# Two transformer blocks on one core: three norms and the query rank are summed by one TensorE tile instead of two, and three warm-up matmuls stand where four stood

## The chip, the cores and the metric

The kernel runs on one core of one Trainium2 chip. The metric is the device time of the program in microseconds (us); lower is better.

## The reference, cut to what matters

Two transformer blocks follow each other over 512 tokens of 1024 features, in float32. The first has latent attention (a query rank of 256 and a key/value rank of 128, each with its own RMS norm), an mLSTM, a gated feed-forward and a gate on per-layer embeddings; the second has differential attention, forgetting attention and a squared-ReLU feed-forward. Every norm has this form:

```python
def rms_norm(x, g):
    xf = x.astype(jnp.float32)
    y = xf * lax.rsqrt(jnp.mean(xf * xf, axis=-1, keepdims=True) + EPS)
    return (y * g.astype(jnp.float32)).astype(x.dtype)

    u = rms_norm(h, attn_pre_norm[i])
    c_q, c_kv, k_rope, ... = split_cols(u @ w_in[i], IN_SIZES)
    q = (rms_norm(c_q, q_norm[i]) @ w_uq[i]).reshape(...)
    ...
    h = h + rms_norm(mix, attn_post_norm[i])
    ...
    x = x + rmsnorm(mix @ w_out[l], ln_attn_post[l])
    ...
    x = x + rmsnorm(u @ w_down[l], ln_mlp_post[l])
```

The change touches how the mean of squares is formed for four of these norms: `cq` (the query rank), `attn_post`, `post_2` and `mlp_post_2` (the three norms behind `w_out`, `w_out_2` and `w_down_2`).

## The kernel before

**Layout.** Features lie on the 128 partitions, tokens along the free axis. A tensor of 1024 features is `KD` = 8 tiles of 128x512 in `tiles` (SBUF). A float32 product is split into three matmuls (`three`, L902 to L904: high x high, low x high, high x low). ScalarE (ACT) rounds the high part, VectorE (DVE) subtracts it to get the low part (L2154, L2157). Weights come as `raw_slab` slabs of 128x1024 by DMA, two slots in turn; ACT makes `w_hi` (L1541), DVE makes `w_lo` (L2154), and TensorE (PE) waits for `slab_lo` before it uses the slab. Almost all time is PE working through these products.

**Order.** Nothing is scheduled automatically. Each engine has its own program, written out by hand, and executes it in order; engines wait for each other by counting semaphores. So a wait on an engine holds up all that stands behind it in that engine's program.

**A norm.** ACT squares each of the 8 tiles into `tiles[SQ]` or `tiles[SQ+1]` (semaphore `sq_done`). DVE adds each square to the sum tile `tiles[SSUM]` (`add_part`, L2207, or `add_square`, L2200; semaphore `ssum_done`). Then PE adds over the partitions: `stat` (from L1006) multiplies each tile of squares, as the stationary operand, with a matrix of ones taken from `cols` (`summed`, L1001; the matmul is L1003), one 128x128 product for each group of 128 tokens. ACT takes the root (L1567), DVE the reciprocal (L2232), and PE spreads the factors over the partitions (`spread`, L1033).

For the norms in `HALVED` (`attn_post`, `post_2`, `mlp_post_2`) the tokens are in two parts, `EARLY` (256 tokens) and `LATE` (256 tokens, norm name with `_b`), so that the early tokens' norm overlaps the late tokens' last matmuls. In these, DVE adds only the first seven tiles of squares. The eighth, `t(SQ + (KD - 1) % 2)`, goes to PE as a second tile, so `stat` issues two products for each 128 tokens and adds them in PSUM.

The query rank has two tiles, `cq0` and `cq1`. DVE copies them out (`rank_taken`), ACT squares them into `early[:, RANK_SQ[0]]` and `[1]` (L1699), and `stat("cq")` multiplies both with ones: 2 tiles x 4 groups of tokens. `stat("ckv")`, for the one tile of the key/value rank, follows at once. Both stand on PE behind the first dense projection (`mq0`) and ahead of the second (`mk0`).

**Start.** While the first weights and activations are loaded, PE multiplies zeros, `WARM` times (L1141), and then begins with `first_of_all` (L942 to L948), the first part of the product `mv`; the rest of `mv` (L902 to L904) goes over the 8 feature tiles k, with a new slab at every even k.

Of the kernel before, what the change touches and what calls it, by code (L numbers as in the profile page):

```python
# [20 lines left out]
ALU = mybir.AluOpType  # L21
# [3 lines left out]
P = 128  # L25
S = 512
ST = S // P
D = 1024
KD = D // P
# [5 lines left out]
ML_H, ML_D, ML_W, TAPS = 4, 128, 512, 4  # L35
# [22 lines left out]
CLAMP = 2.0 ** 58  # L58
OVERFLOWS = 2.0 ** 28.5
SMALLEST = 2.0 ** -50  # L60
WARM = 4


SLAB = 8
# [33 lines left out]
for _name, _n in [("attn_pre_norm", 8), ("attn_post_norm", 8), ("ffn_pre_norm", 8), ("ffn_post_norm", 8),  # L98
# [5 lines left out]
    NCOLS += _n  # L104


NORMS = ([("attn_pre", KD, KD - 1), ("cq", 2, 0), ("ckv", 1, 0), ("ml", ML_H, 0)]
         + [("attn_post", KD, KD), ("attn_post_b", 2, 1), ("ffn_pre", KD, KD - 1), ("ffn_post", KD, KD + 1), ("pre_2", KD, KD - 1)]
         + [("df", DF_H, 0)]
         + [("post_2", KD, KD), ("post_2_b", 4, 3), ("mlp_pre_2", KD, KD - 1), ("mlp_post_2", KD, KD), ("mlp_post_2_b", 1, 0)])  # L110
NORM_NO, SQ0, ADD0, RSTD0 = {}, {}, {}, {}
_sq = _add = NRSTD = 0
for _n, (_name, _t, _a) in enumerate(NORMS):
    NORM_NO[_name], SQ0[_name], ADD0[_name] = _n, _sq, _add
# [6 lines left out]
    _add += _a  # L121
ADDS = {name: a for name, _, a in NORMS}
SQUARES = {name: n for name, n, _ in NORMS}
BY_POOL = {"mlp_post_2": (0, 1, 2, 4, 5, 6), "mlp_post_2_b": (0, 1, 2, 4, 5)}
HALVED = ("attn_post", "post_2", "mlp_post_2")
EARLY, LATE = slice(0, S // 2), slice(S // 2, S)
# [3 lines left out]
def token_tiles(name):  # L130
    return range(ST // 2, ST) if name.endswith("_b") else range(ST // 2) if name in HALVED else range(ST)
# [112 lines left out]
RANK_RAW, RANK_SQ = (4, 5, 6), (12, 13, 14)  # L244
# [37 lines left out]
PROB, MO, TMP, SSUM, SQ, RSTD, NTILES = 0, 4, 8, 10, 11, 13, 14  # L282
# [6 lines left out]
def at(n, it, per):  # L289


    return it * per + n
# [294 lines left out]
def build(nc, xT, pT_in, pos_in, cols_in, square_in, onehot_in, relb_in, stream, out):  # L587
    scratch = nc.dram_tensor("bias_rows", [DF_H, S], F32, kind="Internal").ap()
    decay_rows = nc.dram_tensor("decay_rows", [ML_H, S], F32, kind="Internal").ap()
    with ExitStack() as ctx:  # L590
# [9 lines left out]
        early = nc.alloc_sbuf_tensor_at("early", [P, SET, S], F32, offset=arena_at + -arena_at % 32)  # L600
# [25 lines left out]
        def t(n):  # L626
            return tiles[:, n]
# [7 lines left out]
        sem = Semaphores(lambda name: ctx.enter_context(nc.semaphore(name)))  # L635
# [256 lines left out]
        def _(pe):  # L892
            def claim(key):

                b, before, _ = uses[key]
                if before:
                    pe.wait_ge(*before)
                return bank[b]
# [16 lines left out]
            def u(k):  # L915
                return u_hi[:, k], u_lo[:, k]
# [84 lines left out]
            def summed(o, c, square_, first, last):  # L1001

                return pe.matmul(o[:, c:c + P], square_, ones, start=first, stop=last)  # L1003

            def stat(name):

                o = claim(("stat", name))
                if name == "cq":
                    pe.wait_ge(sem.sq_done, SQ0[name] + 2)
                    for i in range(ST):  # L1010
                        for k in range(2):
                            last = summed(o, i, early[:, RANK_SQ[k], i * P:(i + 1) * P], k == 0, k == 1)
                    last.then_inc(sem.stat_ready, 1)
                    return
                squares = [early[:, RANK_SQ[2]] if name == "ckv" else t(PROB if name in ("ffn_pre", "pre_2", "mlp_pre_2") else SSUM)]
                if ADDS[name]:
                    pe.wait_ge(sem.ssum_done, ADD0[name] + ADDS[name])
                if "post" in name or not ADDS[name]:
                    pe.wait_ge(sem.sq_done, SQ0[name] + SQUARES[name])
                if "post" in name and name != "ffn_post":  # L1020
                    squares.append(t(SQ + (KD - 1) % 2))
                for i in token_tiles(name):
                    for n, square_ in enumerate(squares):
                        last = summed(o, i, square_[:, i * P:(i + 1) * P], n == 0, n == len(squares) - 1)
                last.then_inc(sem.stat_ready, 1)
# [113 lines left out]
            pe.wait_ge(sem.warm_set, 1)  # L1139
            for n in range(WARM):  # L1140
                pe.matmul(bank[STAT_BANK][:, :], warm.to_broadcast([P, P]), warm.to_broadcast([P, S]), start=True, stop=True)  # L1141
# [10 lines left out]
            for n, name in enumerate(DENSE):  # L1152
# [7 lines left out]
                elif n == 7:  # L1160
                    o = claim("gate_cols")
                    pe.wait_ge(sem.gate_scanned, 1)
                    for c in range(2):
                        for i in range(ST):
                            at_ = (c * ST + i) * ML_H
                            last = pe.transpose(o[:, at_:at_ + ML_H], tiles[0:ML_H, TMP + c, i * P:(i + 1) * P], square[0:ML_H, 0, 0:ML_H])
# [172 lines left out]
            for n in range(2):  # L1339
                slot = arrived("proj", n)  # L1340
                for m in range(4):
                    last = features(f"proj{4 * n + m}", slot, 2 * m, [u(6), u(7)])
# [56 lines left out]
            for n in range(KD // 2):  # L1399
                slot = arrived("fv", n)  # L1400
                for k in (2 * n, 2 * n + 1):
                    for i in range(ST):
                        o = claim(f"fv{i}") if k == 0 else bank[uses[f"fv{i}"][0]]
                        x = [part_[:, k, i * P:(i + 1) * P] for part_ in (u_hi, u_lo)]
                        last = three(o[:, :], x, slab(0, slot, (k % 2) * ST, S), k == 0, k == KD - 1)
# [101 lines left out]
            for c, part_ in enumerate(PARTS):  # L1507
                o = claim(("last", c))
                for k in range(HALF2):
# [3 lines left out]
                    last = three(o[:, part_], slab(0, slot, k % SLAB), pair(k, HALF2 + k, cols_=part_), k == 0, k == HALF2 - 1)  # L1513
# [10 lines left out]
            for i in token_tiles("mlp_post_2_b"):  # L1524
                last = summed(late, i * P, t(SQ + (KD - 1) % 2)[:, i * P:(i + 1) * P], False, i == ST - 1)
# [618 lines left out]
        def _(dve):  # L2144
# [8 lines left out]
            def tt(o, a, b, op):  # L2153
                return nc.vector.tensor_tensor(o, a, b, op)  # L2154
# [10 lines left out]
            def slab_lo(s, it=0, step=0):  # L2165

                s += 1
                if isinstance(it, int) and at(s, it, step) >= NSLABS:
                    return
                dve.wait_ge(sem.slab_hi, at(s + 1, it, step))  # L2170
                low(w_lo[:, s % 2], raw[:, s % 2], w_hi[:, s % 2]).then_inc(sem.slab_lo, 1)
# [35 lines left out]
            def add_part(name, n, m, part_):  # L2207

                dve.wait_ge(sem.sq_done, SQ0[name] + n + 1)
                dve.wait_ge(sem.ssum_done, ADD0[name] + n + (not name.endswith("_b")))  # L2210
                tt(tiles[:, SSUM, part_], tiles[:, SSUM, part_], tiles[:, SQ + m % 2, part_], ALU.add).then_inc(sem.ssum_done, 1)
# [13 lines left out]
            def inverse_root(name):  # L2225

                n = RSTD0[name]
                dve.wait_ge(sem.root_done, NORM_NO[name] + 1)
                if name not in ("ml", "df"):
                    i = token_tiles(name)  # L2230
                    own = slice(i[0], i[-1] + 1)
                    nc.vector.reciprocal(rstds[:, n, own], roots[:, n, own]).then_inc(sem.rstd_done, 1)  # L2232
                    return
                every = rstds[:, n:n + 4].rearrange("p h n -> p (h n)")
                if name == "ml":
                    nc.vector.reciprocal(every, every).then_inc(sem.rstd_done, 1)
                    return
                link(nc.vector.reciprocal(every, every))
                stt(every, every, 1.0 / OVERFLOWS, every, ALU.is_gt, ALU.mult).then_inc(sem.rstd_done, 1)
# [219 lines left out]
            o = full(dve, "rg")  # L2459
# [12 lines left out]
            def rank_taken(n):  # L2472
                tt(early[:, RANK_RAW[n]], full(dve, ("cq0", "cq1", "ckv")[n])[:, :], t(RSTD), ALU.mult).then_inc(sem.rank_copied, 1)
# [9 lines left out]
            tt(tiles[low_rows, TMP], tiles[low_rows, TMP], tiles[low_rows, RSTD], ALU.mult).then_inc(sem.rope_added, 1)  # L2483
            slab_lo(SLAB0["ckv"])
            rank_taken(1)
            for n in range(2):
                operand_lo(f"kpe{n}", arena[n * ROPE:(n + 1) * ROPE, A_KPE_L], tiles[low_rows, TMP], arena[low_rows, A_KPE_H])
            dve.wait_ge(sem.gate_log, 1)
# [3 lines left out]
            dve.wait_ge(sem.r_done, 1)  # L2492
            rank_taken(2)
            slab_lo(SLAB0[DENSE[0]])
            dve.wait_ge(sem.operand_lo, SPLIT_NO["kpe1"] + 1)
            link(nc.vector.tensor_tensor_scan(m, r, r, 0.0, ALU.max, ALU.max))
            tt(bm, m, a, ALU.add).then_inc(sem.gate_scanned, 1)
# [24 lines left out]
            for i, name in enumerate(DENSE):  # L2522
# [9 lines left out]
                acc, o = conv_tile(n), conv_input(n)  # L2532
# [138 lines left out]
            for m in range(KD - 2):  # L2671
                out_lo(OUT1, m + 2)
                add_part("attn_post", m, m, slice(0, S))
                if m + 1 < GROUP:
                    aside_lo(FIRST["glu"][m + 1])
            add_part("attn_post", KD - 2, KD - 2, EARLY)
            inverse_root("attn_post")

            def late_attn_post(c, k):
# [236 lines left out]
            def ob(m, c, part_):  # L2916

                o = full(dve, ("ob", m, c))
                if m == 0:
                    dve.wait_ge(sem.part_kept, KD)  # L2920
                tt(tiles[:, m, part_], o[:, part_], part[:, m, part_], ALU.add).then_inc(sem.out_summed, 1)
# [16 lines left out]
            for m in range(5, KD):  # L2938
                ob(m, 0, EARLY)
                add_part("post_2", m - 1, m - 1, EARLY)  # L2940
            ob(4, 1, LATE)
            inverse_root("post_2")
            ob(5, 1, LATE)
# [67 lines left out]
            def last_sum(c, part_):  # L3011

                o = full(dve, ("last", c))
                tt(tiles[:, KD - 1, part_], tiles[:, KD - 1, part_], o[:, part_], ALU.add).then_inc(sem.half_added, 1)

            last_sum(0, EARLY)
            inverse_root("mlp_post_2")
            done = H0["mlp_post_2"]
            for c, (name, part_) in enumerate((("mlp_post_2", EARLY), ("mlp_post_2_b", LATE))):
# [157 lines left out]
```

## Time and profile before

| | |
|---|---|
| time, median of 3 runs | 1284.31 us (1283.98 to 1284.41) |
| the profiled execution | 1284.02 us |
| its span in the profile | 1282.2 us (1.8 us lie around it) |
| PE busy | 1268.9 us, 99% of the span |
| DVE busy | 766.5 us, 60% |
| ACT busy | 549.3 us, 43% |
| chain that ended last | PE 95%, DVE 3%, ACT 1%, issue 1% |

PE is the engine for matmuls and PEld its weight loads, which run beside them. Each float32 product with ones shows as two records, called two passes here: 88 products, 176 records. A record of a matmul includes the way through the array, so that in a train the spacing of the starts, not the duration, says what one costs. The ends of matmuls are modelled.

### The profile page before, as it was taken

To read this page: it belongs to the slowest core of one execution; us is meant where nothing else is said; L and a number is where in the kernel's file an instruction comes from. 1 tells how busy PE (TensorE), PEld (TensorE's weight loads), DVE (VectorE), ACT (ScalarE), POOL (GpSimd) and SP (SyncE) were. 2 spreads that over 40 slices of the span, in tenths; PEclk is the share of its full clock that TensorE was granted. 3 is DMA by queue.
4 is the path that set the end of the run, shared out by engine and by line. 5 is a ranking of instruction groups with operands and counts; after the bars stand their busy time and mean duration, and the time that the engine had idled before them with its cause. 6 is when DMAs were issued, how large, how long until landed. Compare 5 with 4: busy or idle time off the path is not lost.

```text
span 1282.2 us, 17439 instructions
## 1 busy us (share of the span) xinstructions
PE 1268.9 (99%) x6386; PEld 1072.7 (84%) x6386; DVE 766.5 (60%) x1250; ACT 549.3 (43%) x921; POOL 32.5 (3%) x42
## 2 busy tenths in 40 slices
PE   9999999999999999999999999999999999999997
PEld 7887888988888888888888888888988888888886
DVE  6777895655444443323685896898868422455334
ACT  6656865433222223232564655667443222222221
POOL 0010000000000000000000000000000000000002
PEclk9999999999999999999999999999999999999999
DMA  5232113122223223332333323423122322222332
GB/s 199 85 130 83 34 36 130 34 76 89 98 98 98 98 90 124 102 111 98 99 104 110 99 83 93 114 79 112 50 66 85 112 92 92 96 98 98 99 99 82
DMA packets 37563, 120.97 MB, mean 94 GB/s; under 512 B 4600, under 2 KB 6776, under 8 KB 37504
## 3 DMA queue, kind: packets, MB, share of 16 engines
q1 hardware_dynamic: 35888, 116.93, 28.3%
q0 software_dynamic: 896, 2.64, 0.7%
q8 instruction: 39, 0.64, 0.2%
q10 hardware_dynamic: 720, 0.59, 0.1%
q14 instruction: 20, 0.16, 0.0%
HBM read 112.79 MB, written 2.11 MB: 90 GB/s over the span
## 4 chain that ended last, share of the span: by engine, by line
PE 95%; DVE 3%; ACT 1%; issue 1%; DVEq 0%; ACTq 0%
PE bank L902 29%; PE bank L903 29%; PE bank L904 29%; PE bank L1003 2%; PE bank L1096 1%; DVE arena L2157 1%; PE bank L1423 1%; PE bank L1125 0%; PE bank L1141 0%; PE bank L1383 0%; PE bank L1382 0%; DVE tiles L2154 0%; PE bank L1033 0%; PE bank L1073 0%; DVE tiles L2157 0%
## 5 line engine op out<-in xcount | busy, mean ns | idle before, releaser
L2154 DVE TENSOR_TENSOR w_lo<-raw_slab,w_hi 128x1024 fp32r<-128x1024 f32 (+1 forms) x199 | 243.6, 1224 | 269.1 <-ACT w_hi L1541 264.6
L902 PE MATMUL bank<-u_hi,w_hi 128*128 128x512 f32 x824 | 322.8, 392 | 0.0
L904 PE MATMUL bank<-u_hi,w_lo 128*128 128x512 f32 x824 | 321.0, 390 | 0.0
L903 PE MATMUL bank<-u_lo,w_hi 128*128 128x512 f32 x824 | 320.9, 389 | 0.0
L1541 ACT ACTIVATE w_hi<-raw_slab 128x1024 fp32r<-128x1024 f32 x197 | 207.7, 1054 | 183.8 <-PE bank L904 181.3
L902 PE MATMUL bank<-arena,w_hi 128*128 128x512 f32 (+1 forms) x692 | 260.9, 377 | 0.0
L903 PE MATMUL bank<-arena,w_hi 128*128 128x512 f32 (+1 forms) x692 | 259.3, 375 | 0.0
L904 PE MATMUL bank<-arena,w_lo 128*128 128x512 f32 (+1 forms) x692 | 259.3, 375 | 0.0
L904 PEld LDWEIGHTS bank<-u_hi,w_lo 128*128 128x128 f32 x824 | 154.7, 188 | 32.4
L902 PEld LDWEIGHTS bank<-u_hi,w_hi 128*128 128x128 f32 x824 | 154.7, 188 | 31.7 <-issue 0.9
L903 PEld LDWEIGHTS bank<-u_lo,w_hi 128*128 128x128 f32 x824 | 154.8, 188 | 30.7
L904 PEld LDWEIGHTS bank<-arena,w_lo 128*128 128x128 f32 x692 | 130.2, 188 | 23.5
L902 PEld LDWEIGHTS bank<-arena,w_hi 128*128 128x128 f32 x692 | 130.3, 188 | 23.2 <-DVE w_lo L2154 0.3
L903 PEld LDWEIGHTS bank<-arena,w_hi 128*128 128x128 f32 x692 | 130.3, 188 | 22.0
L2154 DVE TENSOR_TENSOR tiles<-tiles 128x512 f32<-128x512 f32 (+2 forms) x129 | 86.6, 672 | 33.3 <-ACT tiles L1826 19.9
L2154 DVE TENSOR_TENSOR tiles<-bank,tiles 128x512 f32<-128x512 f32 (+2 forms) x75 | 51.3, 688 | 65.0 <-PE bank L904 62.1
L2154 DVE TENSOR_TENSOR arena<-tiles,arena 128x512 f32 (+3 forms) x88 | 59.1, 674 | 26.5 <-ACT arena L1875 20.3
L2103 ACT ACTIVATE arena<-tiles 128x512 f32 (+1 forms) x32 | 20.2, 630 | 100.2 <-DVE tiles L2154 100.2
L1654 ACT ACTIVATE tiles<-bank,negmax 128x128 f32<-128x128 f32 (+3 forms) x80 | 41.8, 524 | 36.8 <-DVE negmax L2364 35.7
L1875 ACT ACTIVATE arena<-tiles 128x512 f32 (+1 forms) x22 | 13.9, 632 | 81.5 <-DVE tiles L2154 81.5
L1634 ACT ACTIVATE probsT<-bank 128x128 fp32r<-128x128 f32 (+1 forms) x80 | 35.0, 437 | 24.8 <-PE bank L1096 24.5
L902 PE MATMUL bank<-u_hi,arena 128*128 128x256 f32 (+3 forms) x144 | 42.9, 298 | 0.8 <-DVE u_lo L2157 0.8
(275 smaller groups left out, 1451.5 us busy)
## 6 DMA issues: line engine op xcount, KB each, us to landing
raw_slab<-in_stream SPq DMA_DIRECT2D x197, 512.0 KB, 3.3
aside_raw<-in_stream SPq DMA_DIRECT2D x8, 512.0 KB, 5.2
arena<-arena SPq DMA_DIRECT2D x32, 128.0 KB, 2.3
residual<-in_xT SPq DMA_DIRECT2D x8, 256.0 KB, 5.6
out_hT<-residual SPq DMA_DIRECT2D x12, 128.0 KB, 1.8
arena<-forget_rows SPq DMA_DIRECT2D x8, 128.0 KB, 2.4
raw_slab<-in_stream SPq DMA_DIRECT2D x2, 256.0 KB, 3.3
early<-decay_rows POOLq DMA_DIRECT2D x2, 256.0 KB, 3.8
```

Of the source, the lines that this page charges most:

```text
L902: pe.matmul(o, ws[0], xs[0], start=first, stop=False)
L903: pe.matmul(o, ws[0], xs[1], start=False, stop=False)
L904: return pe.matmul(o, ws[1], xs[0], start=False, stop=last)
L1003: return pe.matmul(o[:, c:c + P], square_, ones, start=first, stop=last)
L1096: last = pe.transpose(o[:, j * P:(j + 1) * P], tiles[:, src, j * P:(j + 1) * P], ident)
L1423: pe.matmul(o[:, 0:w], arena[:, FX_TILES[p][queries][j], i * P:w], arena[:, FX_TILES[p][keys][j], 0:w], start=queries == "q", stop=False)
L1541: nc.scalar.activation(w_hi[:, s % 2], raw[:, s % 2], ACT.Copy).then_inc(sem.slab_hi, 1)
L1634: nc.scalar.activation(transposed(0, v % ST), by_key_tile(o, w), ACT.Copy).then_inc(sem.pT_hi, 1)
L1654: nc.scalar.activation(tiles[:, PROB + exp_slot(a, n, j), 0:w], o[:, 0:w], ACT.Exp, bias=negmax[:, e:e + 1], accum_out=rowsum[:, e:e + 1]) ...
L1875: nc.scalar.activation(arena[:, at(m, it, 2)], t(SQ + m), ACT.Copy).then_inc(sem.hidden_hi, 1)
L2103: nc.scalar.activation(arena[:, at(i, it, 2)], t(SQ + i), ACT.Copy).then_inc(sem.hidden_hi, 1)
L2154: return nc.vector.tensor_tensor(o, a, b, op)
```

## The change

`WARM` goes from 4 to 3. The three halved norms get one more addition on DVE: the eighth tile of squares, early tokens only, is added to `SSUM` as soon as ACT has squared it, and `stat` takes only `SSUM` for the early tokens (the late tokens keep their two tiles). For `cq`, DVE adds the two tiles of squares in place, and `stat` takes the one sum; its wait changes from `sq_done` to `ssum_done`. The numbers in `NORMS` are the count of tiles and of additions.

```diff
-WARM = 4
+WARM = 3
...
-NORMS = ([("attn_pre", KD, KD - 1), ("cq", 2, 0), ("ckv", 1, 0), ("ml", ML_H, 0)]
-         + [("attn_post", KD, KD), ("attn_post_b", 2, 1), ("ffn_pre", KD, KD - 1), ("ffn_post", KD, KD + 1), ("pre_2", KD, KD - 1)]
+NORMS = ([("attn_pre", KD, KD - 1), ("cq", 2, 1), ("ckv", 1, 0), ("ml", ML_H, 0)]
+         + [("attn_post", KD, KD + 1), ("attn_post_b", 2, 1), ("ffn_pre", KD, KD - 1), ("ffn_post", KD, KD + 1), ("pre_2", KD, KD - 1)]
          + [("df", DF_H, 0)]
-         + [("post_2", KD, KD), ("post_2_b", 4, 3), ("mlp_pre_2", KD, KD - 1), ("mlp_post_2", KD, KD), ("mlp_post_2_b", 1, 0)])
+         + [("post_2", KD, KD + 1), ("post_2_b", 4, 3), ("mlp_pre_2", KD, KD - 1), ("mlp_post_2", KD, KD + 1), ("mlp_post_2_b", 1, 0)])
...
             def stat(name):
 
                 o = claim(("stat", name))
-                if name == "cq":
-                    pe.wait_ge(sem.sq_done, SQ0[name] + 2)
-                    for i in range(ST):
-                        for k in range(2):
-                            last = summed(o, i, early[:, RANK_SQ[k], i * P:(i + 1) * P], k == 0, k == 1)
-                    last.then_inc(sem.stat_ready, 1)
-                    return
-                squares = [early[:, RANK_SQ[2]] if name == "ckv" else t(PROB if name in ("ffn_pre", "pre_2", "mlp_pre_2") else SSUM)]
+                ranks = {"cq": RANK_SQ[0], "ckv": RANK_SQ[2]}
+                squares = [early[:, ranks[name]] if name in ranks else t(PROB if name in ("ffn_pre", "pre_2", "mlp_pre_2") else SSUM)]
                 if ADDS[name]:
                     pe.wait_ge(sem.ssum_done, ADD0[name] + ADDS[name])
                 if "post" in name or not ADDS[name]:
                     pe.wait_ge(sem.sq_done, SQ0[name] + SQUARES[name])
-                if "post" in name and name != "ffn_post":
+                if name.endswith("_b"):
                     squares.append(t(SQ + (KD - 1) % 2))
...
             rank_taken(1)
+            rank_squares = early[:, RANK_SQ[0]], early[:, RANK_SQ[1]]
...
             rank_taken(2)
             slab_lo(SLAB0[DENSE[0]])
+            dve.wait_ge(sem.sq_done, SQ0["cq"] + 2)
+            tt(rank_squares[0], rank_squares[0], rank_squares[1], ALU.add).then_inc(sem.ssum_done, 1)
             dve.wait_ge(sem.operand_lo, SPLIT_NO["kpe1"] + 1)
...
             add_part("attn_post", KD - 2, KD - 2, EARLY)
+            add_part("attn_post", KD - 1, KD - 1, EARLY)
             inverse_root("attn_post")
...
                 add_part("post_2", m - 1, m - 1, EARLY)
+            add_part("post_2", KD - 1, KD - 1, EARLY)
             ob(4, 1, LATE)
             inverse_root("post_2")
...
             last_sum(0, EARLY)
+            add_part("mlp_post_2", KD - 1, KD - 1, EARLY)
             inverse_root("mlp_post_2")
```

DVE at the query rank, before. The rows follow each other; `early_50<-bank0` is `rank_taken(2)`, the `w_lo` behind it is the weight slab of `mk0`, and the 4x512 rows are the gates of the mLSTM.

```order
L2154 TENSOR_TENSOR arena<-tiles,arena 64x512 [waits operand_hi] x2
L2157 SCALAR_TENSOR_TENSOR tiles<-tiles 4x512 [waits gate_log]
L2490 SCALAR_TENSOR_TENSOR tiles<-tiles 4x512 [waits dve_step]
L2154 TENSOR_TENSOR tiles<-tiles 4x512 [waits dve_step]
L2154 TENSOR_TENSOR early_50<-bank0,tiles 128x512 [waits slab_used,r_done]
L2154 TENSOR_TENSOR w_lo<-raw_slab,w_hi 128x1024 [waits slab_hi]
L2496 SCALAR_TENSOR_TENSOR tiles<-tiles 4x512 [waits operand_lo]
```

The same place on DVE after the change:

```order
L2148 TENSOR_TENSOR arena<-tiles,arena 64x512 [waits operand_hi] x2
L2151 SCALAR_TENSOR_TENSOR tiles<-tiles 4x512 [waits gate_log]
L2485 SCALAR_TENSOR_TENSOR tiles<-tiles 4x512 [waits dve_step]
L2148 TENSOR_TENSOR tiles<-tiles 4x512 [waits dve_step]
L2148 TENSOR_TENSOR early_50<-bank0,tiles 128x512 [waits slab_used,r_done]
L2148 TENSOR_TENSOR w_lo<-raw_slab,w_hi 128x1024 [waits slab_hi]
L2148 TENSOR_TENSOR early_50<-early_50 128x512 [waits sq_done]
L2493 SCALAR_TENSOR_TENSOR tiles<-tiles 4x512 [waits operand_lo]
```

The new addition stands behind `rank_taken(2)` and behind the low part of the slab.

PE at the query rank, before: the end of `mq0`, the two sums, the start of `mk0`.

```order
L904 MATMUL bank1<-u_hi,w_lo 128x512
L1003 MATMUL bank7<-cols,early_50 128x128 [waits sq_done,rstd_copied]
L1003 MATMUL bank7<-cols,early_50 128x128 x7
L1003 MATMUL bank4<-cols,early_50 128x128 [waits sq_done,rope_read]
L1003 MATMUL bank4<-cols,early_50 128x128 x3
L902 MATMUL bank2<-u_hi,w_hi 128x512 [waits operand_lo,slab_lo]
```

The same place on PE after the change:

```order
L904 MATMUL bank1<-u_hi,w_lo 128x512
L1003 MATMUL bank7<-cols,early_50 128x128 [waits ssum_done,rstd_copied]
L1003 MATMUL bank7<-cols,early_50 128x128 x3
L1003 MATMUL bank4<-cols,early_50 128x128 [waits sq_done,rope_read]
L1003 MATMUL bank4<-cols,early_50 128x128 x3
L902 MATMUL bank2<-u_hi,w_hi 128x512 [waits operand_lo,slab_lo]
```

Eight products with ones became four, and the first of them waits for `ssum_done`.

DVE near the end of the program after the change (`mlp_post_2`), with the new row in the third place. Before the change the same rows stood there without it.

```order
L2148 TENSOR_TENSOR tiles<-tiles 128x512 [waits ssum_done,sq_done]
L2148 TENSOR_TENSOR tiles<-tiles,bank 128x256 [waits part_done]
L2148 TENSOR_TENSOR tiles<-tiles 128x256 [waits ssum_done,sq_done]
L2226 RECIPROCAL rstds<-rstds 128x2 [waits root_done]
L2151 SCALAR_TENSOR_TENSOR tiles<-tiles,cols,bank 128x256 [waits spread_ready]
```

The new addition follows the last sum of tile 7 (`part_done`) and stands ahead of the reciprocal.

## Rows read from the trace of the kernel before

**Rows 1.** The page: busy time by engine, then the chain by engine.

```profile
PE 1268.9 (99%) x6386; PEld 1072.7 (84%) x6386; DVE 766.5 (60%) x1250; ACT 549.3 (43%) x921; POOL 32.5 (3%) x42
...
PE 95%; DVE 3%; ACT 1%; issue 1%; DVEq 0%; ACTq 0%
```

**Rows 2.** Timeline of the start: start us, duration us, engine, line, instruction, [idle before].

```profile
3.65 0.34 PEld L1141 LDWEIGHTS bank<-small 128*128 128x128 f32 x1 [0.52 <-issue]
...
4.51 0.20 PEld L1141 LDWEIGHTS bank<-small 128*128 128x128 f32 x1 [0.52 <-issue]
4.57 0.72 ACT L1666 ACTIVATE u_hi<-residual,cols 128x512 fp32r<-128x512 f32 x1
4.95 0.19 PEld L1141 LDWEIGHTS bank<-small 128*128 128x128 f32 x1 [0.24 <-issue]
...
5.82 0.19 PEld L942 LDWEIGHTS bank<-w_hi,u_hi 128*128 128x128 f32 x1 [0.24 <-issue]
```

**Rows 3.** Timeline, slab 2 of `mv` arrives and feature tile k = 4 begins.

```profile
14.45 1.06 ACT L1541 ACTIVATE w_hi<-raw_slab 128x1024 fp32r<-128x1024 f32 x1 [2.08 <-DMA raw_slab<-in_stream]
...
15.54 1.22 DVE L2154 TENSOR_TENSOR w_lo<-raw_slab,w_hi 128x1024 fp32r<-128x1024 f32 x1 [1.12 <-ACT w_hi L1541]
...
16.95 0.19 PEld L902 LDWEIGHTS bank<-w_hi,u_hi 128*128 128x128 f32 x1
```

**Rows 4.** Timeline, where the engines last wait for PE ahead of the rank.

```profile
34.69 1.06 ACT L1541 ACTIVATE w_hi<-raw_slab 128x1024 fp32r<-128x1024 f32 x1 [0.81 <-PE bank L904]
```

**Rows 5.** Timeline around the two sums of the ranks.

```profile
52.03 0.63 ACT L1699 ACTIVATE early<-early 128x512 f32<-128x512 f32 x1 [3.84 <-DVE early L2154]
...
56.96 2.87 PEld L1003 LDWEIGHTS bank<-cols,early 128*128 128x128 f32 x24
...
57.32 0.69 DVE L2154 TENSOR_TENSOR early<-bank,tiles 128x512 f32<-128x512 f32 x1
57.93 1.22 DVE L2154 TENSOR_TENSOR w_lo<-raw_slab,w_hi 128x1024 fp32r<-128x1024 f32 x1
58.05 0.63 ACT L1699 ACTIVATE early<-early 128x512 f32<-128x512 f32 x1 [3.12 <-DVE early L2154]
59.06 1.21 DVE L2496 TENSOR_TENSOR_SCAN tiles<-tiles 4x512 f32<-4x512 f32 x1
...
59.76 0.19 PEld L902 LDWEIGHTS bank<-u_hi,w_hi 128*128 128x128 f32 x1
```

**Rows 6.** Timeline at the sum of `attn_post`.

```profile
235.13 0.38 ACT L1835 ACTIVATE tiles<-bank 128x256 f32<-128x256 f32 x1 [2.22 <-PE bank L904]
...
236.25 0.98 PEld L1003 LDWEIGHTS bank<-cols,tiles 128*128 128x128 f32 x8
237.16 0.19 PEld L902 LDWEIGHTS bank<-arena,w_hi 128*128 128x128 f32 x1
```

**Rows 7.** Timeline at the sum of `post_2`.

```profile
910.82 0.42 ACT L2056 ACTIVATE tiles<-tiles 128x256 f32<-128x256 f32 x1 [0.85 <-DVE tiles L2154]
...
911.49 0.98 PEld L1003 LDWEIGHTS bank<-cols,tiles 128*128 128x128 f32 x8
```

**Rows 8.** Timeline at the sums of `mlp_post_2`, early and late tokens.

```profile
1265.09 0.42 DVE L2154 TENSOR_TENSOR tiles<-tiles,bank 128x256 f32<-128x256 f32 x1 [2.78 <-PE bank L904]
1265.54 0.42 ACT L2135 ACTIVATE tiles<-tiles 128x256 f32<-128x256 f32 x1 [4.57 <-DVE tiles L2154]
...
1266.21 0.98 PEld L1003 LDWEIGHTS bank<-cols,tiles 128*128 128x128 f32 x8
...
1270.30 0.61 PE L1003 MATMUL bank<-cols,tiles 128*128 128x128 f32 x4
...
1273.30 0.71 PE L1003 MATMUL bank<-cols,tiles 128*128 128x128 f32 x4 [0.96 <-ACT tiles L2135]
```

**Rows 9.** Busy time and granted clock of one stretch, PE first, PEclk behind POOL.

```profile
180.00:190.00 10.00, 8.72 (x65) 7.99 (x64) 9.86 (x25) 6.82 (x20) 0.00 (x0) 1.00 0.07 28
```

**Rows 10.** Who waited for whom, PEld: us in total, times, longest us.

```profile
PEld bank L1003 <- ACT tiles L2135: 1.2, 1, 1.2
```

## Prediction

> **What bounds the kernel now.** I read the page first, then who waited for whom, then the timeline at each place that the diff touches. PE is busy for 99% of the span, and the chain that ended last runs 95% through it [rows 1]. So a microsecond that PE's own program gains or loses is in general one of the span, and work on DVE or ACT costs nothing as long as PE does not wait for it. The question at each place is therefore twofold: how many passes does PE lose, and is DVE's new addition done when PE gets there?
>
> A pass with ones costs what the spacing says. At `attn_post` eight weight loads of L1003 begin at 236.25 and the next product's load at 237.16 [rows 6], so 0.91 / 8 = 0.114 us each. A 128x128 product is two passes.
>
> A wait ahead of such passes costs a little more than its length, since the first weight load is no longer hidden: four passes took 0.61 us where they followed other matmuls and 0.71 us behind a wait [rows 8]. I count 0.10 us for each new wait. From the end of one engine's instruction to the start of one that waited for it there are 0.03 us (DVE ends at 1265.09 + 0.42 = 1265.51, ACT begins at 1265.54) [rows 8].
>
> **Warm-up: about -0.2 us.** At the start the loads of L1141 are 0.86 us apart (3.65 to 4.51), and from 4.51 on 0.44 us (4.51 to 4.95) [rows 2]: TensorE ran at 1.2 GHz there and at 2.4 GHz behind it. The removed matmul is the last one, two passes at the higher level, 0.87 us. What follows can't gain all of it: `u_hi` of the first tile ends only at 4.57 + 0.72 = 5.29 [rows 2], and further on PE meets the DMA. Slab 2 comes late (ACT waited 2.08 us for its DMA), its low part ends at 15.54 + 1.22 = 16.76, and PE takes it at 16.95 [rows 3]. None of that depends on PE, so whatever PE has gained, it can't begin k = 4 before 16.79: a gain of 0.16. The bounds are 0 and 0.4 (the load there may be partly hidden anyway); I take 0.2, near the row's own number. The gain then travels on: ACT waits for PE at 34.69 [rows 4], and DVE's chain up to the rank hangs from there without a pause that could hide 0.2 us.
>
> **The query rank: about +1.9 us.** Four products go, 8 passes. But the addition stands on DVE behind `rank_taken(2)` and the low part of `mk0`'s slab, and DVE begins what now follows those at 59.06 [rows 5]. The squares are long there (52.03 + 0.63 = 52.66), so nothing but the place in the program holds it. The trace has no such addition in `early`, but a DVE tensor-tensor of 128x512 f32 takes 0.69 us here [rows 5]. So `ssum_done` comes at 59.06 + 0.69 = 59.75, and PE's first load at 59.78, where before it stood at 56.96. PE then has the 8 passes of `cq` and the 8 of `ckv`: 16 x 0.114 = 1.82, and 0.10 for the wait: `mk0` begins at 61.70. Before it was 59.76 [rows 5]. That is +1.94. The bounds: +1.5, if DVE's addition is only 0.6 us and the wait costs nothing more, with a DVE that runs somewhat earlier; +2.1 if the passes are spaced as in the whole train of 24 (2.80 / 24 = 0.117) and the restart is slower. Queued behind the wait on PE are `stat("ckv")`, whose own square was ready at 58.05 + 0.63 = 58.68, and all dense projections; the roots and the conversions of later slabs wait for PE in turn. DVE's gate scans move back by 0.6 us. They serve a product of PE six projections later, so that is covered.
>
> **attn_post: -0.45 us.** ACT's square ends at 235.13 + 0.38 = 235.51, DVE is idle, the addition of 128x256 takes 0.42 us (as the sum at 1265.09) [rows 6, 8]: ready at 235.96, ahead of PE's load at 236.25. Four passes go, 4 x 0.114. The cover is 0.29 us; without it the loss would be what it is at the next two.
>
> **post_2: -0.1 us.** The last square ends at 910.82 + 0.42 = 911.24 [rows 7]; with 0.03, the addition 0.42 and 0.03 PE may start at 911.72, and would have at 911.49. So it waits 0.23, plus 0.10, against 0.45 saved: -0.12.
>
> **mlp_post_2: -0.1 us.** The same sum: 1265.54 + 0.42 + 0.03 + 0.42 + 0.03 = 1266.44 against 1266.21 [rows 8], 0.33 lost and 0.45 saved: -0.12. The tail behind PE's last matmuls only moves with it, for its DVE work begins with PE's spread.
>
> The sum: -0.2 + 1.94 - 0.45 - 0.12 - 0.12 = **+1.05 us**. The profiled execution took 1284.02 us, 0.29 below the median of the runs, so it would take 1285.1, and the median **1285.4 us**.
>
> **The rivals.**
>
> *The clock falls in the wait at the rank.* PE would stand still for 59.78 - 57.0, some 2.8 us. The longest wait of PEld that the trace names is 1.2 us [rows 10], and in a stretch in which PE was busy for only 8.72 of 10 us the granted clock read 1.00 [rows 9], so no row shows what a pause of 2.8 us does. If the clock went to 1.2 GHz, the start shows the price: work ran at half rate from 0.93 to 4.51, 3.6 us, half of which, 1.8 us, is lost. That gives +2.85, 1287.2 us, slower. It decides from +2.57 us on. The Trainium skill (TensorE: Matmul & The Clock Gate, Part 1: The HAM clock gate) has the clock fall back to half after TensorE has been idle, and speaks for this case in kind; the pauses that this trace has did not bring it about.
>
> *The shift of the rank is taken up.* In the first attention PE waits for ACT and DVE (8.72 of 10 us busy, DVE 9.86) [rows 9]. If those engines' work there did not hang on PE's delayed products, the 1.94 would vanish there and so would the warm-up's 0.2: -0.7, 1283.6 us. Against it: their inputs are projections that PE makes behind the rank.
>
> *No wait at the rank.* If DVE reached the addition in time, 20 passes at 0.114 = 2.3 us and 0.2 would go: 1281.8 us, just inside the bound, and 1281.2 if the warm-up gave all of its 0.87, faster. Against it stands DVE's order and the row at 59.06.
>
> **How the numbers follow.** A measurement of this kernel tells about 0.2% (2.57 us) from no change. The forecast of +1.05 has a chance of 0.76, the clock 0.10, the shift taken up 0.10, no wait 0.04. The forecast alone spans 1284.4 to 1286.6 by its terms' bounds; to leave out no more than 2 in 10, I reach down to the case of 1283.6 and a little up: 1283.6 to 1286.8. Faster by over 0.2% has 0.03 (part of the last case), slower 0.11 (the clock and the forecast's upper edge), no change 0.86.
>
> **What the profile after would show.** A wait of PEld at L1003 on a DVE addition of some 2.8 us near 57 to 60, and the loads of `mk0` starting at about 61.5 (61.7 less the warm-up's gain); eight passes for `cq` and `ckv` each. Loads 0.22 us apart right behind them, if the clock holds; 0.43 if not. At `attn_post` no wait and four passes; at the other two a wait of some 0.2 us. The first load of k = 4 at about 16.8, with a wait for DVE. Wrong would be the prediction, if the delay at the rank is not found again at the first glu products (near 241.7), or if the passes behind the wait are slower.

## The result and the profile after

The changed kernel takes 1286.79 us (median of 22 runs, 1284.73 to 1287.61); the kernel before, beside it, 1284.59 us (22 runs, 1283.61 to 1285.27). The ratio is 1.0014, with a 95% interval from 1.0008 to 1.0021: slower by 0.14%, about 2 us, but under the 0.2% that I had set as the bound of no change.

The 22 runs are not one group. Seven lie between 1284.73 and 1285.65 us (median 1285.34) with a mean granted clock of TensorE of 0.998 of full speed; fifteen lie between 1286.56 and 1287.61 us (median 1286.87) with 0.996 or 0.997. Nothing lies between. The profiled execution (1285.34 us, span 1283.5) is of the lower group, so its trace shows the change without what makes the upper one. That trace first.

The page of the changed kernel, busy time and chain, answers to [rows 1]:

```profile
PE 1267.2 (99%) x6364; PEld 1069.8 (83%) x6364; DVE 768.4 (60%) x1254; ACT 549.8 (43%) x921; POOL 32.5 (3%) x42
...
PE 93%; DVE 4%; ACT 2%; issue 1%; DMA 0%; SPq 0%; ACTq 0%; DVEq 0%
```

PE has 22 records fewer (10 products with ones and one warm-up matmul, two passes each) and 1.7 us less to do, yet the span is 1.3 us longer. The chain now goes through DVE for 4% instead of 3%.

The timeline of the changed kernel at the query rank (start, duration, engine, line, instruction, [idle before]) answers to [rows 5]:

```profile
57.59 0.69 DVE L2148 TENSOR_TENSOR early<-bank,tiles 128x512 f32<-128x512 f32 x1
...
58.20 1.22 DVE L2148 TENSOR_TENSOR w_lo<-raw_slab,w_hi 128x1024 fp32r<-128x1024 f32 x1
...
59.33 0.69 DVE L2148 TENSOR_TENSOR early<-early 128x512 f32<-128x512 f32 x1
...
60.13 1.86 PEld L1003 LDWEIGHTS bank<-cols,early 128*128 128x128 f32 x16 [2.94 <-issue]
60.16 2.02 PE L1003 MATMUL bank<-cols,early 128*128 128x128 f32 x16 [2.54 <-DVE early L2148]
...
61.91 0.19 PEld L902 LDWEIGHTS bank<-u_hi,w_hi 128*128 128x128 f32 x1
```

The addition is the row at 59.33, behind `rank_taken(2)` and behind the slab, and ends at 60.02. PE's loads stood still for 2.94 us, and its matmuls for 2.54. Sixteen passes then fill 60.13 to 61.91, after which `mk0` begins, 2.15 us later than before. Of these, 0.27 came from the start of the program, so the rank cost 1.9.

The timeline of the changed kernel at `attn_post` and `post_2`, answers to [rows 6, 7]:

```profile
237.71 0.42 DVE L2148 TENSOR_TENSOR tiles<-tiles 128x256 f32<-128x256 f32 x1 [2.46 <-ACT tiles L1829]
238.42 0.54 PEld L1003 LDWEIGHTS bank<-cols,tiles 128*128 128x128 f32 x4
...
912.96 0.43 DVE L2148 TENSOR_TENSOR tiles<-tiles 128x256 f32<-128x256 f32 x1 [0.15 <-ACT tiles L2050]
913.46 0.52 PEld L1003 LDWEIGHTS bank<-cols,tiles 128*128 128x128 f32 x4 [0.21 <-issue]
```

At `attn_post` the new addition is done at 238.13 and PE comes at 238.42 without a pause; at `post_2` PE pauses for 0.21 us. `mlp_post_2` reads like `post_2`, again with 0.21 us.

To see where time goes I use the starts of the sums with ones as marks, since they stand in all versions; they are taken from the chain that ended last, written out in order of time. Each column is a stretch between two of them, so what happened ahead of it drops out: from `attn_pre` to `ml` (it holds the query rank), and from `ml` to the last of `mlp_post_2_b` (it holds the three norms).

| profile | `attn_pre` at | to `ml` | against before | to the last sum | against before |
|---|---|---|---|---|---|
| before | 26.18 | 145.37 | | 1101.75 | |
| after | 26.45 | 147.27 | +1.90 | 1100.91 | -0.84 |

### The profile page after: what moved, and what is told of

It is laid out like the page before. It is cut to its first block, busy times and chain, and to the rows that moved or that the text cites. A ratio compares the mean times of both kernels' runs of the same rounds, so it can differ in the third digit from the quotient of the medians.

```text
span 1283.5 us, 17402 instructions
## 1 busy us (share of the span) xinstructions
PE 1267.2 (99%) x6364; PEld 1069.8 (83%) x6364; DVE 768.4 (60%) x1254; ACT 549.8 (43%) x921; POOL 32.5 (3%) x42
## 4 chain that ended last, share of the span: by engine, by line
PE 93%; DVE 4%; ACT 2%; issue 1%; DMA 0%; SPq 0%; ACTq 0%; DVEq 0%
PE bank L902 28%; PE bank L903 28%; PE bank L904 28%; PE bank L1003 1%; PE bank L1090 1%; DVE tiles L2148 1%; DVE arena L2151 1%; PE bank L1417 1%; DVE w_lo L2148 0%; PE bank L1119 0%; DVE tiles L2151 0%; PE bank L1377 0%; DMA residual<-in_xT 0%; PE bank L1376 0%; PE bank L1067 0%
```

## The experiments

Every time is a median; the kernel before was run beside each. The first four ran on one chip (before: 1284.65 us, 33 runs), the next four on a second (1284.62, 27 runs), the last three on a third (1284.52, 27 runs).

### after_again: the changed kernel, for a profile of the upper group

> The changed kernel once more. Its runs so far lie in two groups, 7 at 1284.7 to 1285.7 us with a mean granted clock of 0.998 and 15 at 1286.6 to 1287.6 us with 0.996 or 0.997; its one profile was of the lower group. Theory A (the clock falls for a while in or behind the wait of 2.9 us that TensorE now has at the query rank): both groups come again, and a profile of the higher group shows matmuls behind the rank 0.43 us apart instead of 0.22, over some 3 us. Theory B (three warm-up matmuls leave TensorE idle for 0.8 us at the start, and the clock rises later): a profile of the higher group is slow at the start, not at the rank.

Measured: 1286.54 us (11 runs; four at 1285.39 to 1285.69, seven at 1286.19 to 1287.35), ratio 1.0012 (1.0003 to 1.0021). The profile, of 1286.19 us, has the mean clock 0.996 of the upper group.

Stretches of this profile, busy time of PE, PEld, DVE, ACT, POOL, then the granted clock, the DMA share and GB/s:

```profile
56.00:60.00 4.00, 1.46 (x7) 0.94 (x6) 3.93 (x6) 2.12 (x3) 0.53 (x1) 0.91 0.02 4
60.00:63.00 3.00, 3.00 (x17) 3.00 (x17) 2.96 (x4) 1.00 (x2) 0.00 (x0) 0.55 0.55 175
63.00:66.00 3.00, 3.00 (x16) 2.46 (x15) 2.13 (x6) 0.97 (x2) 0.00 (x0) 1.00 0.55 168
```

The same stretches of the first profile of the changed kernel, in the lower group:

```profile
56.00:60.00 4.00, 1.62 (x8) 1.00 (x6) 3.93 (x6) 1.66 (x3) 0.53 (x1) 1.00 0.01 4
60.00:63.00 3.00, 2.83 (x21) 2.68 (x22) 2.97 (x5) 2.23 (x4) 0.00 (x0) 1.00 0.49 175
```

And the loads of the sums in the timeline of after_again:

```profile
59.68 3.28 PEld L1003 LDWEIGHTS bank<-cols,early 128*128 128x128 f32 x16 [2.94 <-issue]
62.88 0.19 PEld L902 LDWEIGHTS bank<-u_hi,w_hi 128*128 128x128 f32 x1
```

The wait is the same 2.94 us. But toward its end the clock fell to 1.2 GHz and stayed there for about 3.4 us. (The stretches say so: 0.91 over 4 us is 0.7 us at half speed, 0.55 over 3 us is 2.7 us.) The sixteen passes took 3.20 us (59.68 to 62.88) instead of 1.78 (60.13 to 61.91). From `attn_pre` to `ml` the profile has 148.64 us, 1.37 more than the first one, and the medians of the two groups in the main comparison are 1.53 apart. At the start, where theory B put the cause, this profile is 0.45 us earlier than the other. Theory B falls for this profile; rank_only tests it over several runs. One half of what I expected missed: the slow matmuls are the sums themselves, not the products of `mk0`, for the fall began before the wait was over.

### rank_filled: the wait filled with matmuls over zeros

```diff
             def stat(name):
                 o = claim(("stat", name))
+                if name == "cq":
+                    for n in range(3):
+                        pe.matmul(bank[STAT_BANK][:, :], warm.to_broadcast([P, P]), warm.to_broadcast([P, S]), start=True, stop=True)
```

> The changed kernel with three more matmuls over zeros (128x512, six passes, 2.6 us) on TensorE just ahead of the sum for the query rank, into the bank that the sum then overwrites: they fill the wait and shift nothing, since TensorE would wait there. Theory A: the group at 1286.9 us is gone, all runs near 1285.3 us with clock 0.998. Theory B: both groups stay, 15 of 22 or so in the upper one. If the fill is a little too long, both get up to 0.1 us more.

Measured: 1285.28 us (1285.04 to 1285.71, 11 runs), ratio 1.0005 (0.9996 to 1.0014), the time of the lower group and no run above it. The stretches of its profile:

```profile
56.00:60.00 4.00, 4.00 (x14) 2.45 (x14) 3.90 (x5) 1.28 (x2) 0.52 (x1) 1.00 0.01 4
60.00:63.00 3.00, 3.00 (x21) 2.44 (x20) 2.97 (x5) 2.21 (x5) 0.00 (x0) 1.00 0.56 175
```

PE is now busy throughout, and the clock holds at 1.00; that it held in the other runs too is read from their times. DVE's addition comes as late as ever (147.21 us from `attn_pre` to `ml`, +1.84), only the second price of the wait is gone. It is TensorE standing still that lets the clock fall here, not the lateness of the addition as such.

### rank_sooner: the addition ahead of the slab

```diff
             rank_taken(2)
+            dve.wait_ge(sem.sq_done, SQ0["cq"] + 2)
+            tt(rank_squares[0], rank_squares[0], rank_squares[1], ALU.add).then_inc(sem.ssum_done, 1)
             slab_lo(SLAB0[DENSE[0]])
-            dve.wait_ge(sem.sq_done, SQ0["cq"] + 2)
-            tt(rank_squares[0], rank_squares[0], rank_squares[1], ALU.add).then_inc(sem.ssum_done, 1)
```

> The changed kernel with the addition for the query rank one place earlier on VectorE, ahead of the low part of the slab for mk0 instead of behind it. The addition should end near 58.9 on the scale of the profile after (58.20 + 0.69), not 60.02, so TensorE waits 1.8 us instead of 2.9 and mk0 begins 1.1 us sooner. Theory A: lower group 1284.2 us, and the upper group rarer or gone, since the pause is shorter. Theory B: both groups as often as before, 1.1 us lower. Rival for the wait itself: if the low part of the slab, now 0.6 us later, or the square of the key/value rank ends last, mk0 gains less than 1.1 us.

Measured: 1283.84 us (1283.55 to 1284.24, 11 runs), ratio 0.9994 (0.9985 to 1.0003), one group. The timeline:

```profile
58.17 0.68 DVE L2148 TENSOR_TENSOR early<-early 128x512 f32<-128x512 f32 x1
...
58.97 1.86 PEld L1003 LDWEIGHTS bank<-cols,early 128*128 128x128 f32 x16 [1.80 <-issue]
```

One place on DVE is worth 1.16 us by the marks (146.11 against 147.27), about the slab's 1.13 (58.20 to 59.33 above). With a pause of 1.80 us no run lies in an upper group, and every mean clock is 0.997 or 0.998, so the clock fell in none of the 11. Against the lower group the median is 1.5 lower, 0.4 more than the marks give; that rest is not accounted for, and the start varies by more (below).

### rank_undone: no change at the rank

```diff
-NORMS = ([("attn_pre", KD, KD - 1), ("cq", 2, 1), ("ckv", 1, 0), ("ml", ML_H, 0)]
+NORMS = ([("attn_pre", KD, KD - 1), ("cq", 2, 0), ("ckv", 1, 0), ("ml", ML_H, 0)]
...
+                if name == "cq":
+                    pe.wait_ge(sem.sq_done, SQ0[name] + 2)
+                    for i in range(ST):
+                        for k in range(2):
+                            last = summed(o, i, early[:, RANK_SQ[k], i * P:(i + 1) * P], k == 0, k == 1)
+                    last.then_inc(sem.stat_ready, 1)
+                    return
...
-            dve.wait_ge(sem.sq_done, SQ0["cq"] + 2)
-            tt(rank_squares[0], rank_squares[0], rank_squares[1], ALU.add).then_inc(sem.ssum_done, 1)
```

> The change without its part at the query rank (both tiles of squares go to TensorE again, no addition on VectorE there); three warm-up matmuls and the three norms as changed. From the differences of the two traces the norms give -0.45, -0.2 and -0.2 us. Theory A: no wait, one group of runs, clock 0.998 in all, about 1283.7 us if the start costs nothing, 1284.0 if the shorter warm-up costs the 0.27 us that the profile after showed there. Theory B: two groups 1.5 us apart remain, at 1283.7 and 1285.2.

Measured: 1283.40 us (1282.91 to 1283.57, 11 runs), ratio 0.9991 (0.9981 to 1.0000), one group: 3.1 us below the changed kernel on the same chip (after_again), and 0.3 below the 1283.7 that I expected. The marks say 145.33 and 1100.97: the rank's stretch is back where it was (-0.04), the norms' gain is kept (-0.78).

### rank_later: the addition behind the gate scan

```diff
             link(nc.vector.tensor_tensor_scan(m, r, r, 0.0, ALU.max, ALU.max))
             tt(bm, m, a, ALU.add).then_inc(sem.gate_scanned, 1)
+            dve.wait_ge(sem.sq_done, SQ0["cq"] + 2)
+            tt(rank_squares[0], rank_squares[0], rank_squares[1], ALU.add).then_inc(sem.ssum_done, 1)
```

(The two lines are taken away from their place ahead of the scan.)

> The changed kernel with the addition for the query rank three places later on VectorE, behind the two steps of the gate scan: it should begin 1.8 us later, so TensorE waits some 4.7 us instead of 2.9 and the lower group would be at 1287.2 us. Theory A: the clock falls in every run and, since the wait is longer, mostly while TensorE stands still, so the time is between 1287.5 and 1289 us with no run in a group of 0.998. Theory B: 1287.2 and 1288.7 us as often as before.

Measured: 1288.96 us (1288.54 to 1289.98, 6 runs), ratio 1.0033 (1.0021 to 1.0046). No run has a clock above 0.996. The loads of the sums and three stretches of its profile, which is of the slowest of the six runs:

```profile
61.82 3.49 PEld L1003 LDWEIGHTS bank<-cols,early 128*128 128x128 f32 x16 [4.77 <-issue]
...
60.00:63.00 3.00, 1.15 (x5) 1.18 (x6) 2.97 (x5) 1.05 (x1) 0.00 (x0) 0.70 0.48 175
63.00:66.00 3.00, 3.00 (x15) 2.90 (x14) 0.68 (x3) 0.62 (x3) 0.00 (x0) 0.50 0.44 168
66.00:69.00 3.00, 3.00 (x11) 2.34 (x10) 2.37 (x4) 0.61 (x1) 0.00 (x0) 0.66 0.02 7
```

The pause is 4.77 us here, and the clock stays down about twice as long as in after_again, about 6.8 us by the same working, well into `mk0`. The median lies at the upper edge of the 1287.5 to 1289 us that I expected, and for another reason: I had the clock low mostly while TensorE stands still, but it fell only at 61.2 us, 0.6 us ahead of the load at 61.82, and nearly all of the low stretch was work. The stretch from `attn_pre` to `ml` has 152.03 us in this profile, +6.66 against before. The wait itself explains about 3.7 (1.9, and 1.8 for the later place), the clock the other 2.9.

### rank_only: the rank's change on the kernel before, four warm-up matmuls

The diff is the rank's part of the change alone: `("cq", 2, 1)`, the new `squares` for `cq` in `stat`, and the addition on DVE.

> The kernel before with the change at the query rank alone, four warm-up matmuls. Theory A: two groups of runs, one 1.9 us above the kernel before (1286.5 us), one a further 1.4 to 1.6 us up (1288.0 us), though the warm-up is the old one. Theory B (the warm-up makes the upper group): one group only, at 1286.5 us.

Measured: 1287.98 us (10 runs; three at 1285.69 to 1285.83, seven at 1287.94 to 1288.72), ratio 1.0022 (1.0013 to 1.0032). The two groups are there with the old warm-up, and their medians are 2.3 apart. So the shorter warm-up does not make them: theory B falls here for good. Its profile (1288.10 us) has 148.84 us from `attn_pre` to `ml`, +3.47 and near after_again's +3.27, so the clock's share at the rank is at most 0.2 us larger here; that the lower group lies 0.7 below the 1286.5 I expected is not explained by a profile, since none was taken in it.

### warm_only: three warm-up matmuls, nothing else

```diff
-WARM = 4
+WARM = 3
```

> The kernel before with three warm-up matmuls instead of four and nothing else. Theory A (what follows the warm-up soon waits for the DMA of slab 2, so only 0.2 to 0.3 us arrive): a median 0.2 to 0.4 us below the kernel before, one group of runs. Theory B (the shorter warm-up costs, since TensorE idles before its first real matmul): 0.3 us or more above it, or a second group of runs some 1.5 us higher.

Measured: 1283.71 us (1283.31 to 1284.59, 11 runs) against 1284.62, 0.9 us lower where I expected 0.2 to 0.4; the ratio, 0.9996 (0.9987 to 1.0005), does not by itself tell it from no change. Theory B, that the shorter warm-up costs time or makes a second group, has nothing for it: the 11 runs have no group 1.5 us up. A likely reason why it gave more than I expected is in the next profile.

### norms_only: the three norms, four warm-up matmuls

The diff is that of the three norms: `KD + 1` in `NORMS`, `name.endswith("_b")` in `stat`, and the three `add_part(..., KD - 1, KD - 1, EARLY)`.

> The kernel before with the change to the three norms alone (four warm-up matmuls, query rank as before). By the marks in the traces the parts give 0.45, 0.2 and 0.2 us: 0.85 us below the kernel before, so near 1283.8 us. If the extra additions on VectorE cost TensorE more elsewhere than at these places, the gain is below 0.5 us. With rank_undone at 1283.4 us, the difference between the two is the warm-up's share.

Measured: 1283.94 us (1283.06 to 1284.48, 11 runs), 0.7 us below the kernel before, ratio 0.9994 (0.9985 to 1.0003). The marks give 145.38 and 1100.92 us: -0.83 from the norms and nothing at the rank. And its profile, of the slowest of the 11 runs, shows what the one profile of before did not: a start in which the clock rose late.

```profile
3.65 0.34 PEld L1142 LDWEIGHTS bank<-small 128*128 128x128 f32 x1 [0.52 <-issue]
4.51 0.34 PEld L1142 LDWEIGHTS bank<-small 128*128 128x128 f32 x1 [0.52 <-issue]
5.36 0.34 PEld L1142 LDWEIGHTS bank<-small 128*128 128x128 f32 x1 [0.52 <-issue]
6.21 0.34 PEld L1142 LDWEIGHTS bank<-small 128*128 128x128 f32 x1 [0.52 <-issue]
6.98 0.19 PEld L942 LDWEIGHTS bank<-w_hi,u_hi 128*128 128x128 f32 x1 [0.43 <-issue]
...
9.96 0.19 PEld L902 LDWEIGHTS bank<-w_hi,u_hi 128*128 128x128 f32 x1
```

The loads are 0.85 us apart until 6.21, where in [rows 2] they are 0.44 apart from 4.51 on. So the fourth warm-up matmul ran almost wholly at the lower level (5.36 to 6.98, 1.6 us for its two passes), and the first real matmul's load came at 6.98 instead of 5.82, though its operands were ready before 5.4. In the profile of warm_only it comes at 5.46:

```profile
4.17 0.19 PEld L1141 LDWEIGHTS bank<-small 128*128 128x128 f32 x1 [0.24 <-issue]
5.46 0.76 PEld L942 LDWEIGHTS bank<-w_hi,u_hi 128*128 128x128 f32 x4 [1.10 <-ACT w_hi L1669]
```

### best_again, norms_warm2, norms_warm0: how many warm-up matmuls

All three are rank_undone, with `WARM` at 3, 2 and 0.

> The version with three warm-up matmuls and the three norms changed, query rank as before, once more beside shorter warm-ups on one chip: 1283.4 us again, 0.8 to 1.3 us below the kernel before, in one group.

> The same with two warm-up matmuls (four passes, which end near 4.3 us while the clock is still at its lower level in most profiles). The first real matmul can't start before 5.3 us in any case (the activations are rounded then). Theory A (a warm-up matmul costs only where it runs past 5.3 us, and the clock needs work ahead of it to rise): no gain against three, and where the clock has not risen the pause of 1 us lets it rise later: 1283.4 to 1285 us. Theory B (warm-up matmuls are only in the way): 1283.0 us or less.

> The same with no warm-up matmuls. Theory A: the first real matmuls run at the lower level from 5.4 us on until the clock rises, some 3 to 7 us later; but the DMA of slab 2 hides a part of the 1.7 to 3.4 us that this costs, so 1284 to 1287 us. Theory B: 1283.0 us or less.

| `WARM` | us, median of 11 | range | ratio to before |
|---|---|---|---|
| 3 | 1283.39 | 1282.82 to 1283.95 | 0.9990 (0.9981 to 0.9999) |
| 2 | 1284.00 | 1283.01 to 1284.75 | 0.9995 (0.9986 to 1.0004) |
| 0 | 1284.28 | 1283.64 to 1285.31 | 0.9998 (0.9989 to 1.0007) |

The timeline of norms_warm0 at its first matmuls:

```profile
5.45 1.35 PEld L942 LDWEIGHTS bank<-w_hi,u_hi 128*128 128x128 f32 x4 [5.45 <-issue]
6.90 1.61 PEld L945 LDWEIGHTS bank<-w_lo,u_hi 128*128 128x128 f32 x4
8.60 0.97 PEld L948 LDWEIGHTS bank<-w_hi,u_lo 128*128 128x128 f32 x4
```

The first eight real matmuls run at about half speed there (3.15 us from 5.45 to 8.60, against 1.74 from 5.46 to 7.20 in the profile of warm_only), but the median is only 0.9 us above that with three. I take it that the waits for data that follow at the start give the rest back; no run tests that. All three lie where I expected them (with 2 and 0 by theory A); theory B, with 1283.0 us or less for both, falls. Three is the best of the counts tried, by medians whose ranges overlap. The version with three, the norms changed and the rank as before, is the fastest of the study: 1283.40 and 1283.39 us on two chips, 1.1 to 1.3 us (0.1%) below the kernel before, and 3.1 below the changed one on the same chip.

## Why the prediction was right, and where it was not

**The time lay in the range and the class was right, but the likeliest case was not the commonest.** I forecast 1285.4 us from a sum of +1.05 and gave the fall of the clock a chance of 1 in 10. The sum describes the lower group (1285.34 us) to within 0.1. But 15 of 22 runs were of the rival, 1286.87 us, and these set the median, which rose by 2.2 us where I had +1.05. That 1286.79 lies in my range at all is luck: the range ends at 1286.8, and the bounds that I named for the terms add up to no more than +1.7, which is 1286.1 us and not the 1286.6 that I gave. The rest was padding, and the rival's own 1287.2 us I had left outside. One sign that I named for being wrong, slower passes behind the wait, came in the upper group. The step that failed is the weight given to that rival. I had its mechanism, its place and the gap of 2.8 us in hand (2.94 measured), but took the 1.2 us pauses of the trace and a clock of 1.00 in them as evidence against it, though they said nothing about a pause over twice as long. Its price was 1.4 to 1.5 us, not 1.8: of the 3.4 us at the lower level in after_again 0.4 passed while TensorE was still idle, and half of the other 3.0 is 1.5.

**The rank, +1.94 predicted.** +1.90 by the marks in the lower group. The place on DVE's program decided it: the addition at 59.33 on the new scale, 0.27 later than 59.06, as the start was. Without the wait the loads would have begun at 57.23 (56.96 and the 0.27), so they came 2.90 late; the 24 passes had taken 2.80 (56.96 to 59.76) and the 16 took 1.78, so 1.02 of it was saved again.

**attn_post, -0.45 predicted.** From its sum to that of `attn_post_b` 6.86 us before and 6.41 after (236.53 to 243.39, 238.70 to 245.11): -0.45.

**post_2 and mlp_post_2, -0.12 each predicted.** -0.17 and -0.18. The marks must stand on both sides of the pause: from the sum ahead of `post_2`'s to that behind it 126.70 us before and 126.53 after (794.38 to 921.08, 796.06 to 922.59), at `mlp_post_2` 322.66 and 322.48 (947.80 to 1270.46, 949.31 to 1271.79). The pause came as predicted in kind (0.21 us). The 0.10 us that I charged for each restart was too much: the four passes took 0.68 us there, against 0.61 unhindered, so 0.07; that and a pause 0.02 shorter explain the 0.05 by which I was off.

**The warm-up, -0.2 predicted.** The term was mis-sized, and the profile after shows the sign reversed: PE reached `attn_pre` 0.27 us later than before. Its loads of `w_lo,u_hi` at L945 were 0.67 us ahead (6.28 against 6.95), and that went in three waits that the start before did not have, most of it in the first:

```profile
8.76 0.19 PEld L902 LDWEIGHTS bank<-w_hi,u_hi 128*128 128x128 f32 x1 [0.71 <-issue]
...
11.77 0.19 PEld L902 LDWEIGHTS bank<-w_hi,u_hi 128*128 128x128 f32 x1 [0.44 <-DVE w_lo L2148]
...
17.28 0.19 PEld L902 LDWEIGHTS bank<-w_hi,u_hi 128*128 128x128 f32 x1 [0.19 <-DVE w_lo L2148]
```

What came late was mostly what DMA brought: ACT began on the activations of the second tile at 7.13 instead of 6.51. The last wait is that for slab 2, the one that I had foreseen at 16.8; ACT could take the slab only at 14.90 instead of 14.45, and in other profiles between 14.07 and 15.26. So one pair of profiles says nothing of this term: `attn_pre` comes between 25.58 and 26.99 us in the eight profiles with three warm-up matmuls, and at 26.18, 26.73 and 27.35 in the three with four. In the medians the shorter warm-up is worth more than I said (-0.9 in warm_only, -0.5 between norms_only and rank_undone, on different chips). I had read the clock's rise at 4.51 from one profile; it comes at another time in each execution, and where it comes late the fourth matmul costs 1.6 us (norms_only), not 0.87.

**The other rivals.** The shift of the rank was not taken up anywhere: +1.90 at `ml` is still there at the end, less what the norms gave. And DVE did not reach the addition in time.

What stays open is what decides, for one and the same wait of 2.94 us, whether the clock falls (22 of 33 runs of the changed kernel). The runs show that it depends on the length: none of 11 runs at 1.80 us, two thirds at 2.94, all 6 at 4.77. The traces hold a hint. Finer stretches, of after_again, rank_only and rank_later in this order, put the three falls at 59.28, 60.32 and 61.22 us:

```profile
59.20:59.40 0.20, 0.00 (x0) 0.00 (x0) 0.20 (x1) 0.20 (x1) 0.00 (x0) 0.70 0.00 0
60.00:60.50 0.50, 0.05 (x1) 0.08 (x1) 0.50 (x2) 0.48 (x2) 0.00 (x0) 0.82 0.00 0
61.00:61.50 0.50, 0.00 (x0) 0.00 (x0) 0.50 (x2) 0.05 (x1) 0.00 (x0) 0.72 0.96 377
```

The traces' records of the clock have the first rise at 4.67, 5.71 and 6.61 us in these, so each fall comes 54.6 us behind the first rise, though the pauses began within 0.8 us of each other. The moment at which the clock can fall thus seems tied to the first rise, which differs by execution, and what decides would be how far the pause has got by then. In the profile of the lower group the rise is at 4.38; the same distance ends at 58.99, earlier in the pause than in the three, and the clock held; in rank_sooner (rise at 5.63) it ends at 60.24, when TensorE had been at work again since 58.97. These five profiles fit; no run tests it.

The gap of 2.3 us between rank_only's groups, against 1.5 in the changed kernel, is open too, but the same hint would cover it. With four warm-up matmuls a late rise also puts off the first real matmul (5.82 us in before, 6.40 in rank_only, 6.98 in norms_only, for rises at 4.5, 5.7 and 6.9), so there the runs whose clock falls at the rank would also have started later.

## What to carry to other kernels

Work that is moved from a full engine to one with time to spare is only free at the place where it lands: follow the idle engine's program and read when it gets there, for being 60% busy says nothing about the next 3 us. A wait on TensorE has two prices, its length and the clock behind it, and the second can come in some executions only; so look at the spread of the runs and at each run's granted clock, and take a profile from each group before explaining a median. A start-up effect read from a single profile should be given the spread of several.

## What the runs showed of the hardware

- TensorE's clock fell from 2.4 to 1.2 GHz toward the end of a pause of 2.94 us and stayed down for about 3.4 us (after_again, rank_only), toward the end of one of 4.77 us and for about 6.8 us (rank_later). By their times and mean clocks this happened in two thirds of the runs at 2.94 us, in all 6 at 4.77 and in none of 11 at 1.80. With matmuls over zeros in the pause it happened in none of 11. The Trainium skill (TensorE: Matmul & The Clock Gate, Part 1: The HAM clock gate) has the clock halve after an idle stretch; the traces agree, and add that one and the same pause can let it fall in some executions of a kernel and not in others.
- The granted clock in the profile reads 1.00 in the first microseconds, although the passes there are 0.85 us apart, twice the 0.43 behind the rise: at the start the spacing is to be trusted, not the column (0.00 to 4.00 us of before and of norms_only).
- The moment of the first rise differs by execution: in the spacing of the warm-up passes it lies at about 3.9 us (warm_only), 4.5 us (before), 5.7 us (rank_only) and 6.9 us (norms_only) of the span.
